# A hybrid decoder block: the mixing stage's first tile and branch weights read in attention's last head, the residual rows read during the last experts

## The chip, the cores and the metric

The kernel runs on one NeuronCore of a Trainium2 chip. The metric is the time of one execution on the device in microseconds, as the median of several runs. The core has five engines that run side by side and meet at semaphores: TensorE (PE; PEld is its weight load), VectorE (DVE), ScalarE (ACT), GpSimd (POOL) and SyncE (SP), which here only issues DMAs.

## The reference

One decoder block on 2048 tokens of width 1024, in f32, followed by a last norm:

```python
h = rmsnorm(x, g_mix)
proj = h @ w_in
attn = mla_attention(...)                 # 8 heads, causal
conv = gated_short_conv(bcx, conv_w)
mixed = g_a * (attn @ w_branch_a) + g_b * (conv @ w_branch_b)
x = x + mixed @ w_out
x = x + memory_cross_attention(rmsnorm(x, g_xattn), rmsnorm(mem, g_mem), ...)
x = x + hierarchical_moe(rmsnorm(x, g_moe), ...)   # 64 experts, two per token
return rmsnorm(x, g_final)
```

## The kernel before

The kernel is a chain of stages, each a block of its own: at its end all engines meet, and the next stage's instructions start together. The stages that matter here are `attention`, `mix`, `experts` and `combine`. Precise products are made of three TensorE products: each operand is cast to a high half (ACT), and the rest is subtracted out as a low half (DVE or POOL); high by high, high by low and low by high are summed in PSUM.

`attention` goes through 8 heads. A head has 40 steps `u`, one tile of scores each (128 keys by up to 512 queries, in four query chunks). Per step TensorE makes the scores three steps ahead and the products with the values two steps behind, ACT makes two exponentials, and DVE (odd steps) or POOL (even steps) subtracts the low half `pl`. In all heads but the last, DVE also finds the maxima of the next head (`top`). ACT copies each finished chunk out of PSUM (`copy_out`, at steps 8, 16, 28 and step 4 of the next head), and SP stores it to `o_d` (values) and `l_d` (row sums) in DRAM. SP's list is in order: the stores, the loads of the next head, the two small writes of the maxima. Before the first head the keys and values of the memory are computed from a 32 KB region per partition (`ea_both`) that `front` had used, and staged through `kmT` and `vm`.

`mix` has 8 chunks of 256 tokens (`CM`). Per chunk TensorE makes 16 groups of 12 products (`branches`, L1139: for each of 8 feature tiles `j` one group with the convolution tile `cT` and `w_branch_b`, one with the attention tile `aT` and `w_branch_a`), then 4 groups of 24 (`output`, L1155, with `w_out`). DVE multiplies each branch group by its gate (L1259) and adds the pair (L1261), ACT casts the sum (L1195), POOL takes its low half (L1225), DVE adds the residual rows (L1270). The attention tile is divided by its row sums (`divide`: a reciprocal of 128x1024 at L1240, a product at L1242), cast by ACT (L1178) and lowered by POOL (L1213). Of the gates four tiles stand in slots, each refilled when its pair is done.

Ahead of the first chunk the weights are brought in: 16 parts of 512 KB (4 of `w_branch_b`, 4 of `w_branch_a`, 8 of `w_out`) go through four staging slots (the halves of `xr` and `xo`). ACT casts each (L1170), DVE lowers the first eight (L1247), POOL the last eight (L1220), and SP issues a part when the slot of the part four before is free. The first convolution, `ar` and `lr` tiles are issued behind part 3, the gates behind part 7, the first residual rows behind part 15. TensorE's first branch group waits for four low halves, the second for eight, the first output group for all of `w_out`.

`experts` goes through 64 experts. The weights of one (two parts of gate and up, one of down, 1 MB each) lie in one of four slots of `raw` (12 MB in all); SP refills the first two parts when DVE has lowered them, the third when the down product is done (L2021). POOL gathers the tokens' rows and scatters the results to `y_d` by indirect DMA (L2061). For the last four experts nothing is refilled.

`combine` goes through 16 tiles of 128 tokens. For each, SP loads the residual rows (512 KB, `cb_xr`, L2301) and the two experts' rows (1 MB, `cb_ys`, L2302) into four slots, and the gain row once, behind the first four pairs. DVE adds both expert rows with their weights (L2345, L2347), ACT squares, sums and takes the root (L2368, L2370), DVE inverts and multiplies (L2352, L2356), SP stores (L2306).

## Time and profile before

| | us |
|---|---|
| median of the runs | 3069.8 (3068.3 to 3072.6) |
| profiled execution | 3075.1 |
| its span | 3073.3 |

| engine | busy us | share |
|---|---|---|
| PE | 2710.8 | 88% |
| DVE | 1604.7 | 52% |
| ACT | 1281.2 | 42% |
| POOL | 627.1 | 20% |

The profile counts time from the start of the span. `attention` ends and `mix` opens at about 1428 us, `mix` ends about 1831, the experts end near 2974 and `combine` runs to the end. A line of the timeline gives the start, the duration, the engine, the line of the kernel, the operation and its operands with their form, how many of them in a row it stands for, and in brackets the idle time before it with the one who ended it. Granted clock and DMA share are given by stretch of time.

### The profile page before, as it was taken

The page shows a single profiled execution, that of the slowest core. Times are in us where ns is not written, and L with a number is a line of the kernel's source. Part 1 is how long each engine was busy: PE and PEld are TensorE (multiplying, and loading weights), DVE is VectorE, ACT ScalarE, POOL GpSimd, SP SyncE. Part 2 cuts the span into 40 slices and gives each one's busy share as a digit, 9 for nine tenths or more (in the row PEclk, how much of TensorE's full clock was granted, in tenths as well). Part 3 has the DMA queues.
Part 4 walks back from the last instruction along what each step waited for, and adds up shares of the span by engine and source line. Part 5 has one row for each costly group of instructions (what it writes and reads, how often), then busy time and mean ns, then how long its engine had stood idle before and what let it go on. Part 6 is the DMA issues. An engine that isn't in the chain of part 4 may idle for free. (4 is left out here: it accounts for less than half of the span.)

```text
span 3073.3 us, 37486 instructions
## 1 busy us (share of the span) xinstructions
PE 2710.8 (88%) x12695; PEld 2070.6 (67%) x12695; DVE 1604.7 (52%) x2108; ACT 1281.2 (42%) x2105; POOL 627.1 (20%) x710
## 2 busy tenths in 40 slices
PE   7999999999979999995899985999729999999960
PEld 5787777777746666664899974777516777666630
DVE  3624525325245666653444423554466777676637
ACT  4334333333317766665211113443205555555524
POOL 0000000000015555553422210000012222344410
PEclk9999999999989999997999996999859999999985
DMA  4353452452531112203544523222256999999958
GB/s 160 99 179 120 134 161 96 163 198 80 179 78 36 39 35 43 56 9 108 162 117 127 150 84 135 74 103 89 83 203 238 361 360 360 359 365 358 349 202 355
DMA packets 168444, 507.57 MB, mean 165 GB/s; under 512 B 40560, under 2 KB 69488, under 8 KB 140176
## 3 DMA queue, kind: packets, MB, share of 16 engines
q1 hardware_dynamic: 149904, 472.59, 44.8%
q0 software_dynamic: 18432, 33.60, 3.0%
q8 instruction: 61, 1.00, 0.1%
q14 instruction: 47, 0.39, 0.0%
HBM read 431.19 MB, written 108.33 MB: 176 GB/s over the span
## 5 line engine op out<-in xcount | busy, mean ns | idle before, releaser
L485 DVE TENSOR_TENSOR fr_wl<-fr_raw,fr_wh 128x1024 fp32r<-128x1024 f32 x128 | 156.8, 1225 | 469.0 <-ACT fr_wh L356 468.6
L2230 DVE TENSOR_TENSOR ex_gl<-ba_raw,ex_gh 128x2048 fp32r<-128x2048 f32 x128 | 290.7, 2291 | 152.7 <-ACT ex_gh L2161 152.7
L356 ACT CAST fr_wh<-fr_raw 128x1024 fp32r<-128x1024 f32 x128 | 134.0, 1047 | 490.6 <-PE fr_acc L280 490.6
L2161 ACT CAST ex_gh<-ba_raw 128x2048 fp32r<-128x2048 f32 x128 | 241.0, 1906 | 95.1 <-DMA ba_raw<-in_w_exp 52.9
L898 ACT ACTIVATE at_pf<-at_psS 128x512 f32<-128x512 f32 (+1 forms) x320 | 178.5, 559 | 168.8 <-PE at_psS L783 86.0
L1006 POOL TENSOR_TENSOR at_pl<-at_pf,at_ph 128x512 fp32r<-128x512 f32 (+1 forms) x160 | 194.8, 1218 | 263.1 <-ACT at_ph L899 262.6
L2125 PE MATMUL ex_psY<-ba_raw,ex_hT 128*128 128x512 f32 x512 | 232.0, 596 | 9.8 <-issue 8.8
L2104 PE MATMUL ex_psG<-ex_gh,ex_xh 128*128 128x512 f32 x512 | 225.6, 441 | 2.9 <-DVE ex_hm L2241 1.4
L969 DVE TENSOR_TENSOR at_pl<-at_pf,at_ph 128x512 fp32r<-128x512 f32 (+2 forms) x160 | 144.1, 904 | 147.8 <-ACT at_ph L899 144.8
L930 DVE TENSOR_REDUCE at_nm<-at_psA 128x1 f32<-128x512 f32 (+2 forms) x320 | 183.1, 605 | 66.5 <-PE at_psA L817 44.0
L2106 PE MATMUL ex_psG<-ex_gh,ex_xl 128*128 128x512 f32 x512 | 201.5, 393 | 0.0
L2105 PE MATMUL ex_psG<-ex_gl,ex_xh 128*128 128x512 f32 x512 | 201.0, 392 | 0.0
L899 ACT ACTIVATE at_ph<-at_psS 128x512 fp32r<-128x512 f32 (+1 forms) x320 | 177.3, 554 | 0.0
L1155 PE MATMUL mx_psO<-mx_wo,mx_mT 128*128 128x512 f32 x768 | 175.6, 389 | 0.0
L982 POOL CAST at_vh<-all_cst 128x32 fp32r<-128x32 f32 x2 | 0.5, 226 | 856.6 <-POOLq L109 856.6
L2125 PEld LDWEIGHTS ex_psY<-ba_raw,ex_hT 128*128 128x128 f32 x512 | 92.2, 190 | 106.0 <-issue 105.8
L1155 PEld LDWEIGHTS mx_psO<-mx_wo,mx_mT 128*128 128x128 f32 x768 | 143.7, 188 | 29.5
L280 PE MATMUL fr_acc<-ea_hh,fr_wh 128*128 128x512 f32 x512 | 137.8, 412 | 2.0 <-DVE ea_hl L503 2.0
L280 PE MATMUL fr_acc<-fr_hh,fr_wh 128*128 128x512 f32 x512 | 137.0, 410 | 2.9 <-DVE fr_wl L485 2.9
L817 PE MATMUL at_psA<-at_kh,at_qh 96*128 96x512 f32 (+2 forms) x320 | 119.8, 431 | 20.6 <-DVE at_nm L930 17.4
L780 PE MATMUL at_psS<-at_qh,at_kh 98*128 98x512 f32 (+1 forms) x320 | 122.9, 384 | 9.7 <-DMA at_qh<-at_ml 7.6
L1139 PE MATMUL mx_psAB<-mx_cT,mx_wb 128*128 128x256 f32 x768 | 105.3, 288 | 27.6 <-POOL mx_cT L1211 19.1
(320 smaller groups left out, 5891.6 us busy)
## 6 DMA issues: line engine op xcount, KB each, us to landing
ba_raw<-in_w_exp SPq DMA_DIRECT2D x192, 1024.0 KB, 18.6
fr_raw<-in_w_slabs SPq DMA_DIRECT2D x128, 512.0 KB, 4.2
gates_d<-fr_gst SPq DMA_DIRECT2D x64, 256.0 KB, 4.6
mx_gt<-gates_d SPq DMA_DIRECT2D x64, 256.0 KB, 5.6
cb_ys<-y_d SPq DMA_DIRECT2D x16, 1024.0 KB, 9.3
xa_xe<-x_d SPq DMA_DIRECT2D x18, 512.0 KB, 5.5
mx_xr<-in_x SPq DMA_DIRECT2D x8, 1024.0 KB, 7.1
x_d<-mx_xo SPq DMA_DIRECT2D x8, 1024.0 KB, 5.1
```

The source lines that it names most:

```text
L280: mm = nc.tensor.matmul(acc[i % 2][:], w[:, i % 2, k, :], h[q % 2][:, k, :], start=(j == 0 and k == 0), stop=(j == 2 and k == KD - 1))
L898: nc.scalar.activation(pf[:, u % PR, off:CH], psS[u % RING][:, off:CH], ACT.Exp)
L899: nc.scalar.activation(ph[:, u % PR, off:CH], psS[u % RING][:, off:CH], ACT.Exp).then_inc(hi, 1)
L930: V.tensor_reduce(nm[:, i, c:c + 1], psA[b][:, 0:w], AX, ALU.max, negate=True).then_inc(a_max, 1)
L1006: G_.tensor_tensor(pl[:, r, off:CH], pf[:, r, off:CH], ph[:, r, off:CH], ALU.subtract).then_inc(lo[0], 1)
L1155: mm = nc.tensor.matmul(psO[n][:], mT[:, x_, k, q * P:(q + 1) * P], wop[:, y_, k, hf * CH:(hf + 1) * CH], start=(k == 0 and i == 0), stop= ...
L2104: nc.tensor.matmul(psG[s][:], xh[:, s, f, :], gh[:, s, i, k, :], start=(f == 0), stop=False)
L2105: nc.tensor.matmul(psG[s][:], xh[:, s, f, :], gl[:, s, i, k, :], start=False, stop=False)
L2106: mm = nc.tensor.matmul(psG[s][:], xl[:, s, f, :], gh[:, s, i, k, :], start=False, stop=(f == KD - 1))
L2125: mm = nc.tensor.matmul(psY[f][:], hT[:, s, k, :], raw[:, r, 2, k * D + f * CH:k * D + (f + 1) * CH], start=(k == 0), stop=(k == 1))
L2161: nc.scalar.copy(gh[:, s, i], raw[:, r, i, :].rearrange("p (k n) -> p k n", k=KD // 2)).then_inc(w_hi, 1)
L2230: V.tensor_tensor(gl[:, s, i], raw[:, r, i, :].rearrange("p (k n) -> p k n", k=KD // 2), gh[:, s, i], ALU.subtract).then_inc(w_lo, 1)
```

## The change

Five things, in one edit:

1. In the last head of `attention` SP reads both branch weights (2 MB each) into `wb_raw` and `wa_raw`, which lie in the 32 KB region that the memory's key and value weights had; then, once the first chunk of the last head is stored, `ar` and `lr` of the first mixing tile, into the place of `kmT` and `vm`. DVE makes the reciprocal in four quarters (steps 24 to 30) and the product (step 32), ACT casts it (step 34), POOL lowers it (step 36) into `aT`, which lies over `memT`.
2. `mix` no longer stages the branch weights: ACT casts them from `wb_raw` and `wa_raw`. The low halves of `w_out` (`wo_lo`) lie in the same 32 KB region, so they wait for the eighth low half.
3. The low halves of `w_out` are made by DVE, one behind each feature tile of the first chunk; ACT casts parts 12 to 15 among its casts of that chunk. The first chunk is written out apart from the loop (`chunks_first`). SP issues the convolution tile first, then parts 8 and 9, the gates, parts 10 and 11, then 12 to 15 as low halves free the slots; the first residual rows and the next chunk's inputs come behind the last low half.
4. In the last three experts SP reads the residual rows of `combine` (8 reads of 1 MB) into slots of `raw` as they come free.
5. `combine` takes the residual rows from there, has six slots for the expert rows and three for the output, loads the gain row behind the first tile, and is written out without loops.

The core of the diff:

```diff
@@ attention, SP
-            head(H - 1, 1, False, False, True)
-            store(H - 1, 3)
+            sp.dma_start(wb_raw[:], w_b.rearrange("(k p) n -> p k n", p=P)).then_inc(mixer["ab_in"], 16)
+            sp.dma_start(wa_raw[:], w_a.rearrange("(k p) n -> p k n", p=P)).then_inc(mixer["ab_in"], 16)
+            store(H - 2, 3)
+            store(H - 1, 0)
+
+            sp.wait_ge(o_st[0], 64 * H)
+            sp.wait_ge(kv_out, 32)
+            sp.dma_start(ar[:], o_d[:, 0:CM].rearrange("(f p) t -> p f t", p=P)).then_inc(mixer["ar_in"], 16)
+            for e in range(2):
+                sp.dma_start(lr[e * VD:(e + 1) * VD, :, :], l_d[e:H:2, 0:CM].unsqueeze(0).broadcast_to([VD, H // 2, CM])).then_inc(mixer["ar_in"], 16)
+            for c in range(1, NC_):
+                store(H - 1, c)
@@ attention, ACT, DVE, POOL
+                    if not more and u == 34:
+                        act.wait_ge(mixer["divided"], 1)
+                        nc.scalar.copy(aT[:, 0], ar[:]).then_inc(mixer["in_hi"], 1)
+                    if not more and u in (24, 26, 28, 30):
+                        f = (u - 24) // 2
+                        dve.wait_ge(mixer["ar_in"], 48)
+                        V.reciprocal(lr[:, f, :], lr[:, f, :]).then_inc(mixer["inverted"], 1)
+                    if not more and u == 32:
+                        dve.wait_ge(mixer["inverted"], 4)
+                        V.tensor_tensor(ar[:], ar[:], lr[:], ALU.mult).then_inc(mixer["divided"], 1)
+                    if not more and u == 36:
+                        pool.wait_ge(mixer["in_hi"], 1)
+                        G_.tensor_tensor(aT[:, 1], ar[:], aT[:, 0], ALU.subtract).then_inc(mixer["a_lo"], 1)
@@ mix, SP
-            for i in range(PARTS):
+            conv(0)
+            for i in range(8, PARTS):
                 if i >= 12:
-                    sp.wait_ge(w_lo_p, i - 11)
+                    sp.wait_ge(w_lo, i - 3)
...
-                if i == 7:
+                if i == 9:
                     for j in range(4):
                         gates(0, j)
...
+                if first:
+
+                    sp.wait_ge(w_lo, PARTS)
+                    xrows(0)
@@ mix, ACT and DVE
+                    if first and 2 <= j < 6:
+                        high(10 + j)
...
+                    if first:
+                        low(8 + j)
@@ experts, SP
+            for j in range(NT // 2):
+                r, i = 1 + j // 3, j % 3
+                e = E - RAW + r
+                if i < 2:
+
+                    sp.wait_ge(w_lo, 2 * e + i + 1)
+                else:
+                    sp.wait_ge(down, e + 1)
+                sp.dma_start(raw[:, r, i, :].rearrange("p (t d) -> p t d", d=D),
+                             x3_d[2 * j * P:2 * (j + 1) * P, :].rearrange("(t p) d -> p t d", p=P)).then_inc(x3_in[j], 16)
@@ combine, SP
-    R = 4
+    R = 6
...
+            load(0)
             sp.dma_start(gb[:], g.broadcast_to([P, D])).then_inc(g_in, 16)
+            for i in range(1, R):
+                load(i)
+            for i in range(NT):
+                if i + R < NT:
+                    load(i + R)
+                store(i)
```

## Rows read from the trace of the kernel before

**Rows 1.** Waits of TensorE, 1425 to 1810: who for whom, us, times, longest

```profile
PE mx_psAB L1139 <- POOL mx_cT L1211: 19.1, 1, 19.1
PE mx_psAB L1139 <- DVE mx_wa L1247: 15.0, 1, 15.0
PE mx_psAB L1139 <- DVE mx_m L1259: 8.5, 1, 8.5
```

**Rows 2.** Timeline of TensorE, mixing: start, duration, line, operands, count, idle before

```profile
1443.58 2.90 PE L1139 MATMUL mx_psAB<-mx_cT,mx_wb 128*128 128x256 f32 x12 [19.14 <-POOL mx_cT L1211]
...
1494.77 21.95 PE L1155 MATMUL mx_psO<-mx_wo,mx_mT 128*128 128x512 f32 x96
1516.56 1.60 PE L1139 MATMUL mx_psAB<-mx_cT,mx_wb 128*128 128x256 f32 x12
```

**Rows 3.** Waits of DVE in `combine`, 2975 to the end, columns as rows 1

```profile
DVE cb_xr L2345 <- DMA cb_gb<-in_g_final: 19.3, 1, 19.3
DVE cb_xr L2345 <- DMA cb_ys<-y_d: 10.0, 12, 1.0
```

**Rows 4.** Stretches: busy per engine (count), then TensorE's clock, DMA share, GB/s

```profile
2955.00:2975.00 20.00, 11.88 (x39) 6.47 (x37) 2.29 (x5) 2.19 (x6) 3.71 (x7) 0.96 0.13 51
2975.00:2994.00 19.00, 0.00 (x0) 0.00 (x0) 0.00 (x0) 1.19 (x1) 0.00 (x0) 0.50 0.90 359
...
3015.00:3060.00 45.00, 0.00 (x0) 0.00 (x0) 35.60 (x37) 18.46 (x33) 0.00 (x0) 0.50 1.02 422
```

**Rows 5.** Timelines of SP, DVE, POOL and TensorE, attention's last head to mixing's start

```profile
1370.25 0.59 SPq L716 DMA_DIRECT2D at_qh<-at_ml  x1
...
1383.92 0.51 SPq L721 DMA_DIRECT2D o_d<-at_ost  x1
...
1404.48 0.69 DVE L969 TENSOR_TENSOR at_pl<-at_pf,at_ph 128x512 fp32r<-128x512 f32 x1 [3.14 <-ACT at_ph L899]
...
1421.02 0.74 POOL L1006 TENSOR_TENSOR at_pl<-at_pf,at_ph 128x256 fp32r<-128x256 f32 x1 [0.72 <-ACT at_ph L899]
...
1423.74 0.28 PE L799 MATMUL at_psO<-at_ph,at_vh 128*66 128x256 f32 x1
...
1428.22 1.20 SPq L1084 DMA_DIRECT2D mx_xr<-in_w_branch_b  x2
```

**Rows 6.** DMA issues of mixing, whole span: count, KB each, median us to landing

```profile
mx_gt<-gates_d SPq DMA_DIRECT2D x64, 256.0 KB, 5.6
...
mx_cv<-conv_d SPq DMA_DIRECT2D x8, 512.0 KB, 5.7
...
mx_lr<-l_d SPq DMA_DIRECT2D x16, 256.0 KB, 9.1
```

**Rows 7.** Timelines of DVE, SP and POOL in mixing's steady chunks

```profile
1675.06 6.54 DVE L1240 RECIPROCAL mx_lr<-mx_lr 128x1024 f32<-128x1024 f32 x1
...
1709.23 0.45 SPq L1062 DMA_DIRECT2D mx_ar<-o_d  x1
...
1729.28 2.40 POOL L1213 TENSOR_TENSOR mx_aT<-mx_ar,mx_aT 128x1024 fp32r<-128x1024 f32 x1 [5.45 <-ACT mx_aT L1178]
```

**Rows 8.** Timelines of DVE and POOL before mixing's first chunk

```profile
1454.66 2.35 DVE L1247 TENSOR_TENSOR mx_wa<-mx_xr,mx_wa 128x1024 fp32r<-128x1024 f32 x2
1456.93 4.50 DVE L1247 TENSOR_TENSOR mx_wa<-mx_xo,mx_wa 128x1024 fp32r<-128x1024 f32 x2
...
1455.90 3.31 POOL L1213 TENSOR_TENSOR mx_aT<-mx_ar,mx_aT 128x1024 fp32r<-128x1024 f32 x1 [12.43 <-ACT mx_aT L1178]
```

**Rows 9.** Line L2061, the last three scatters, 2950 to 2974

```profile
L2061 POOL DMA_INDIRECT y_d<-ex_y,ex_iy x3: 992/993/996, 2955.5 to 2970.1; - x3
...
DMA to landing us min/median/max: 3.2/3.2/3.2
```

**Rows 10.** Line L2061, four scatters among the weight loads, 2900 to 2935

```profile
DMA to landing us min/median/max: 9.0/9.5/10.0
```

**Rows 11.** Timeline of DVE in `combine`, the first sums of two tiles

```profile
3000.95 1.28 DVE L2345 SCALAR_TENSOR_TENSOR cb_xr<-cb_ys,ba_wts,cb_xr 128x1024 f32<-128x1024 f32 x1
...
3004.97 1.28 DVE L2345 SCALAR_TENSOR_TENSOR cb_xr<-cb_ys,ba_wts,cb_xr 128x1024 f32<-128x1024 f32 x1
```

More of the change, by code:

```diff
@@ L22 @@
 CH = 512
+CM = 256
 NC_ = T // CH
@@ L1076, in _, with chunk @@
             sp.sem_inc(stored, 16)
-            for i in range(PARTS):
+            conv(0)
+            for i in range(8, PARTS):
                 if i >= 12:
-                    sp.wait_ge(w_lo_p, i - 11)
-                elif i >= 4:
-                    sp.wait_ge(w_lo_v, i - 3)
+                    sp.wait_ge(w_lo, i - 3)
                 stage, src, _hi, _lo = weight(i)
                 sp.dma_start(stage, src).then_inc(w_in[i % 4], 16)
-                if i == 3:
-                    conv(0)
-                    rows(0)
-                if i == 7:
+                if i == 9:
                     for j in range(4):
                         gates(0, j)
-            sp.wait_ge(w_lo_p, PARTS - 8)
-            xrows(0)
-            def chunk(c, more):
-                here = sp.snap(c + 0) if more else c
-                after = sp.snap(c + 1) if more else None
+            def chunk(c, more, first=False):
+                here = sp.snap(c + 0) if more and not first else c
+                after = sp.snap(c + 1) if more and not first else c + 1
                 for j in range(4):
@@ L1115, in chunk @@
                     xrows(after)
-            chunks(sp, chunk)
+            chunks_first(sp, chunk)
             sp.wait_ge(stored, 16 * NM + 16)
@@ L1144, in output @@
                 if first:
-                    pe.wait_ge(w_lo_p, PARTS - 8)
+                    pe.wait_ge(w_lo, PARTS)
                 for n in range(2 * NQ):
@@ L1184, in _, with chunk @@
                 high(i)
-            attention_high(0)
-            for i in range(8, PARTS):
+            for i in range(8, 12):
                 high(i)
-            def chunk(c, more):
+            def chunk(c, more, first=False):
                 for j in range(KD):
@@ L1200, in chunk @@
                     attention_high(c + 1)
-            chunks(act, chunk)
+            chunks_first(act, chunk)
         @block.gpsimd
@@ L1215, in _ @@
             pool.sem_inc(m_lo, 2)
-            inputs(0)
-            for i in range(8, PARTS):
-                pool.wait_ge(w_hi, i + 1)
-                stage, _src, hi, lo = weight(i)
-                G_.tensor_tensor(lo, stage, hi, ALU.subtract).then_inc(w_lo_p, 1)
+            conv_low(0, 2)
             def chunk(c, more):
@@ L1240, in divide, with low, chunk @@
                 V.reciprocal(lr[:], lr[:]).then_inc(inverted, 1)
-                dve.wait_ge(inverted, c + 1)
+                dve.wait_ge(inverted, c + 4)
                 V.tensor_tensor(ar[:], ar[:], lr[:], ALU.mult).then_inc(divided, 1)
-            for i in range(8):
+            def low(i):
                 dve.wait_ge(w_hi, i + 1)
                 stage, _src, hi, lo = weight(i)
-                V.tensor_tensor(lo, stage, hi, ALU.subtract).then_inc(w_lo_v, 1)
-                if i == 3:
-                    divide(0)
-            def chunk(c, more):
+                if i == 8:
+                    dve.wait_ge(w_lo, 8)
+                V.tensor_tensor(lo, stage, hi, ALU.subtract).then_inc(w_lo, 1)
+            for i in range(8):
+                low(i)
+            def chunk(c, more, first=False):
                 for j in range(KD):
@@ L1964, in _, with experts @@
             link(V.tensor_copy(meta[:, 0:32], psK[0:1, 0:32]))
-def experts(nc, cst, h_d, w_exp, y_d, tab, rows, meta, raw, r_in):
+def experts(nc, cst, h_d, x3_d, w_exp, y_d, tab, rows, meta, raw, r_in, x3_in):
     with ExitStack() as ctx:
@@ L2362, in _ @@
             act.wait_ge(eps_set, 1)
[L2363 to L2370 removed]
+            for i in range(NT):
+                act.wait_ge(added, i + 1)
+                if i >= 2:
+                    act.wait_ge(rcp_done, i - 1)
+                nc.scalar.activation(sq[:], x_tile(i), ACT.Square, accum_out=st[:, i % 2, 0:1]).then_inc(sq_done, 1)
+                act.wait_ge(sq_done, i + 1)
+                nc.scalar.activation(st[:, i % 2, 1:2], st[:, i % 2, 0:1], ACT.Sqrt, bias=eps[:], scale=1.0 / D).then_inc(rms_done, 1)
 def program(nc, a, out):
@@ L2407, in program @@
                   a["mem"], a["g_mem"], a["w_kv_mem"], hh0, hl0, wk_mem, wv_mem, memT, kv_in)
-            attention(nc, cst, qn_d, qr_d, kn_d, kr_d, v_d, o_d, l_d, wk_mem, wv_mem, memT, kv_in, km_d, vm_d)
-        mix(nc, o_d, l_d, conv_d, gates_d, x, a["w_branch_a"], a["w_branch_b"], a["w_out"], x2_d)
+            at = -(-nc.sbuf_base // 32) * 32
+            kmT, vm = e_.sb("kmT", [P, XH, MEM]), e_.sb("vm", [P, MEM // P, XH * XD])
+            ar, lr = (e_.at(n, [P, 4, CM], F32, at + 4 * 4 * CM * i) for i, n in enumerate(("ar", "lr")))
+            attention(nc, cst, qn_d, qr_d, kn_d, kr_d, v_d, o_d, l_d, wk_mem, wv_mem, memT, kmT, vm, kv_in, km_d, vm_d,
+                      a["w_branch_a"], a["w_branch_b"], wb_raw, wa_raw, ar, lr, aT, mixer)
+            mix(nc, o_d, l_d, conv_d, gates_d, x, a["w_out"], x2_d, wb_raw, wa_raw, wo_lo, ar, lr, aT, mixer)
         clear_semaphores(nc)
@@ L2432, in program @@
             route(nc, cst, lg, wts, tab, rows, meta, load_first_experts)
-            experts(nc, cst, h_d, a["w_exp"], y_d, tab, rows, meta, raw, r_in)
-            combine(nc, x3_d, y_d, wts, a["g_final"], out)
+            x3_in = [b_.sem(f"x3_in{i}") for i in range(NT // 2)]
+            experts(nc, cst, h_d, x3_d, a["w_exp"], y_d, tab, rows, meta, raw, r_in, x3_in)
+            combine(nc, raw, x3_in, y_d, wts, a["g_final"], out)
 def constants():
```

140 lines of the change are left out of this document (66 added, 74 removed).

## The prediction

> **What bounds the kernel now.** I read the waits first, then the timeline where they are long. In the mixing stage TensorE stands still three times, 19.1, 15.0 and 8.5 us, and never again [rows 1]: first for POOL's low half of the convolution tile, then for DVE's low halves of `w_branch_a`, then for DVE's `mx_m`, which itself was held by POOL working through the low halves of `w_out`. TensorE's groups show it: the first twelve products at 1443.58, the first output products at 1494.77, the second chunk at 1516.56 [rows 2]; from there the stage runs on TensorE without a gap. In `combine` DVE waits 19.3 us once, for the gain row that is queued behind four pairs of loads, then 10.0 us in twelve waits for the expert rows [rows 3]. The DMA share by stretch says why: 0.13 in the last 20 us of the experts, then 0.90 and 1.02 [rows 4]. So both ends of this change aim at time in which TensorE or DVE really waits. The profiled execution took 3075.1 us (span 3073.3); the median of the runs is 3069.8, 5.3 below it. I sum in the profile's clock and take the gain off the median.
>
> **Part 1, the last head of attention.** Added there: on SP two reads of 2 MB (the branch weights), one read of `ar`, two of `lr`; on DVE four reciprocals of a quarter each and one product; on ACT one cast; on POOL one subtraction. SP issues the weights behind the maxima of head 7, at 1370.9 [rows 5]. At 359 GB/s [rows 4] 4.2 MB take 12 us, so they are in by 1383. Head 6's last store, now queued behind them, lands about then; ACT needs it only at step 16 of the head, near 1392. The chain that matters: the first store of head 7 is issued at 1383.9 [rows 5], SP waits for its landing (about 3 us), then issues `ar` and `lr`, whose median landing is 9.1 us [rows 6], so about 1398. DVE asks for them behind step 23, about 1401, and its next piece of attention work starts at 1404.48 after 3.14 us of idle [rows 5]: a quarter of the reciprocal (6.54 us whole [rows 7]), 1.6 us, fits in. The later gaps on DVE are about as wide. ACT's cast and DVE's product lie two units of work or more ahead of TensorE. Only POOL is tight: its subtraction of 2.40 us [rows 7] comes behind step 36 and ahead of its last piece, which ran at 1421.02 for 0.74 us; it now ends near 1423.5, and TensorE starts those products at 1423.74 [rows 5]. I take a loss of 0.5 us (0 to 3). Cover gone: any lateness of the read beyond 1404.5 stops DVE, and with it TensorE, one for one.
>
> **Part 2, the start of mixing.** The block opens at 1428.22 as before [rows 5]. ACT casts the four parts of `w_branch_b` at once (about 1 us each), waits for the convolution tile, now the first DMA, landing 5.7 us after issue [rows 6], so 1434, then casts `w_branch_a`. DVE's low halves take 1.18 us each (two in 2.35) [rows 8]. While POOL subtracts the convolution tile DVE is held for about 1.4 us, so the eighth low half is done near 1442. TensorE's first group starts near 1438.5 at the lower clock (2.90 us against 1.60 for twelve products [rows 2]), its second at 1442 instead of 1461.5. From then on a pair of groups takes 2.9 us, and DVE has per pair two products, one sum and now one low half, about 2.5 us: it keeps up until the fourth pair.
>
> Then a new wait. SP issues `w_out` parts 12 to 15 only as the low halves 8 to 11 free the slots, one per pair, and only behind part 15 the gates of pair 4. The pairs end at 1443.9, 1446.8, 1449.7 and 1452.6, and the sum and low half of the fourth take 2.4 us more, so with SP's issues that is near 1455.5; the gates land 5.6 us after issue [rows 6], so 1461.1, while DVE wants them at 1455.6. From there DVE sets the pace: two products, one sum (about 1.15 us together), one low half (1.2 us) and what POOL's subtraction costs it. The rows for that: two low halves that met a POOL subtraction took 4.50 us instead of 2.35, and POOL's took 3.31 us instead of 2.40 [rows 7, 8]. Each held the other. Here POOL's piece is about 0.7 us long and has to wait for ACT's cast, while DVE's low half starts right behind the sum; so DVE mostly goes first, and between nothing and 0.7 us I take 0.1. Four pairs of 2.45 us give 9.8 us: all sixteen low halves are done at 1471, and the output products start there, not at 1494.77. TensorE idles about 4.5 us before them; I charge 1 us for the low clock (0 to 1.5, half of a cold 2.90).
>
> The Trainium skill (SBUF — State Buffer, section "Who interferes with whom") says that a DVE instruction with two SBUF inputs and a POOL instruction that reads SBUF exclude each other, and that the later one waits the whole earlier one out. If POOL came first in all four pairs, that rule would make this sum 2.5 us longer; the rows above agree with it in kind.
>
> **Part 3, the second chunk's inputs.** They move behind that new wait too: SP may fetch the x rows, then `conv`, `ar`, `lr` only once all low halves are done. In steady state 22.4 us pass from the issue of `ar` (1709.23) to the end of POOL's low half (1731.68) [rows 7]. Here 0.9 us of other issues and 1 MB of x rows (2.9 us at 359 GB/s) come on top: 1471 + 26.2 = 1497.2. TensorE ends the output products 21.8 us [rows 2] plus the 1 us after 1471, at 1493.8, and needs the half one group later, 1495.3. A new stall of about 1.8 us (0 to 4). Gain of the stage: 1516.6 - 1493.8 - 1.8 = 21 us; with the gates in time it is 27, with both chains at their long ends 13. The seven later chunks are the same code.
>
> **Part 4, the residual rows.** Eight reads of 1 MB go out when slots of the last three experts come free: two near 2933, three near 2953.6, three near 2963.6, into a DMA that is 0.13 busy [rows 4]; nothing of the experts' own weights is behind them. What they meet is POOL's scatter. It lands 3.2 us after issue when alone [rows 9], 9.5 under full weight traffic [rows 10]. The last three megabytes are through by about 2974, so the last scatter (issued at 2970) shares only part of its time: I take 1.5 us on the end of the block (0 to 6.3). The Trainium skill (DMA: Bandwidth & Descriptors, "Queues, rings and completion order") says that each DMA engine takes turns between queues by the packet. With turns the scatter pays the 1.5; without them it would stand behind the reads, at most 3.
>
> **Part 5, combine.** The first expert rows are now alone in front: issue 2976.3, landing about 4.8 us later, 2981.1; the gain row and the second tile (1.5 MB, 4.2 us) give 2985.3, where DVE waits 1.6 us. Against 2994.0 (2974.7 + 19.3 [rows 3]) that is 11.3 us. Then each tile needs 1.5 MB instead of 2: at 422 GB/s [rows 4] 3.7 us, below DVE's own 4.02 us a tile (3000.95 to 3004.97 [rows 11]), so the twelve waits, 10.0 us, go. Straight code drops the register work of a loop; I take 1.5 us (0 to 2). ACT's two table loads stay beside the start. Gain 11.3 + 10.0 + 1.5 = 22.8, call it 23. What is late next is DVE.
>
> **Sum.** 21 + 23 - 0.5 = 43.5 us: 3031.6 on the profile's scale, 3026 against the median.
>
> **Rivals.** (a) The gates are no wait: they come in time because DVE is later or because they land in 3 us. Mixing gains 26: 3021. For it: two parts of `w_out` may have drained by then. Against: they stand last in SP's order. Chance 0.13. (b) `combine` turns DMA-bound: reads and stores mixed move 360 GB/s as in the read-only stretch, 4.37 us a tile, 15 x 0.35 = 5 us lost: 3031. Against it stands the 422 of the same loop. Chance 0.14. (c) Mixing keeps a long start: DVE, which now has all sixteen low halves, loses the full POOL time and the second chunk's inputs come late; gain 13: 3034. Chance 0.10. (d) The change does less than it says: both (b) and (c), with 6 us on the last scatter: 3045. Chance 0.05. (e) Slower: the read of `ar` and `lr` in the last head. SP waits for a store that stands behind 4 MB, and DVE waits for the read with TensorE's products behind it. Each us beyond 1404.5 costs one; the gain is eaten when the read lands later than 1447, 60 us after its issue. At 1460 it gives 3082. Rows show 9.1 us for such a read, so 0.04, a fifth of it landing near no change.
>
> **Chances.** Forecast 0.54. Cases (a), (b), (c) and the forecast hold 0.91; with the unknown costs at their ends they reach from 3015 to 3040, which I give as the range. A measurement of this kernel can tell some 0.2%, 6 us. Faster 0.95, same 0.01, slower 0.04.
>
> **What would show it.** In the profile after: the first TensorE group of mixing near 1438, the second near 1442; a DVE wait for `mx_gt` of some 5 us near 1456; first output products near 1471; a wait of TensorE for POOL's `mx_aT` near 1496. In `combine`, no wait for the gain row, first sum about 6.5 us after the block opens, DVE back to back at 4 us a tile. Wrong would be: waits of DVE for `at`'s read in the last head, waits for the expert rows on most tiles, or the last scatter landing more than 5 us after issue.

## The result, and the profile after

The changed kernel takes 3022.6 us (median of four runs, 3015.9 to 3024.7) against 3070.2 us (3068.3 to 3072.6) beside it on the same chip: a ratio of 0.985, 95% interval 0.983 to 0.986, so 47.7 us faster. The forecast was 3026 (3015 to 3040). The profiled execution took 3024.7 us, its span is 3022.9.

The first lines of its page: TensorE is busy for as long as before (2707.9 us against 2710.8) in a shorter span.

```profile
span 3022.9 us, 37234 instructions
## 1 busy us (share of the span) xinstructions
PE 2707.9 (90%) x12695; PEld 2067.9 (68%) x12695; DVE 1611.0 (53%) x2119; ACT 1270.1 (42%) x2098; POOL 607.0 (20%) x702
```

The waits of TensorE from 1365 to 1560 (for whom, us, times, longest), the answer to [rows 1]:

```profile
PE mx_psAB L1165 <- POOL mx_cT L1240: 11.4, 1, 11.4
PE mx_psAB L1165 <- DVE mx_m L1291: 2.5, 1, 2.5
PE mx_psO L1181 <- DVE ea_wo_lo L1278: 2.1, 1, 2.1
PE mx_psAB L1165 <- DVE mx_wa L1278: 1.5, 1, 1.5
```

The timeline of TensorE behind it, the answer to [rows 2]: first group, second group, first output products, second chunk.

```profile
1435.05 2.90 PE L1165 MATMUL mx_psAB<-mx_cT,mx_wb 128*128 128x256 f32 x12 [11.41 <-POOL mx_cT L1240]
1439.49 2.93 PE L1165 MATMUL mx_psAB<-ea_aT,mx_wa 128*128 128x256 f32 x12 [1.54 <-DVE mx_wa L1278]
...
1469.44 0.73 PE L1181 MATMUL mx_psO<-mx_wo_hi,mx_mT 128*128 128x512 f32 x2 [2.11 <-DVE ea_wo_lo L1278]
...
1492.95 1.59 PE L1165 MATMUL mx_psAB<-mx_cT,mx_wb 128*128 128x256 f32 x12
1494.82 1.70 PE L1165 MATMUL mx_psAB<-ea_aT,mx_wa 128*128 128x256 f32 x12 [0.27 <-POOL ea_aT L1246]
```

The wait of 15.0 us for `w_branch_a` is 1.5, the one of 8.5 for `mx_m` is 2.5. The block now opens at 1427.10, so the second chunk starts 65.9 us behind the opening instead of 88.3 (1516.56 less 1428.22 in [rows 2, 5]). The new waits stand on DVE: timeline, the gates of pair 4, the place where they were issued on SP, and the first reads for the second chunk.

```profile
1459.36 0.76 DVE L1291 TENSOR_TENSOR mx_m<-mx_psAB,mx_gt 128x256 f32<-128x256 f32 x2 [5.75 <-DMA mx_gt<-gates_d]
...
1454.01 1.97 SPq L1100 DMA_DIRECT2D mx_gt<-gates_d  x4
1469.41 0.37 SPq L1103 DMA_DIRECT2D mx_xr<-in_x  x1
1469.83 0.46 SPq L1097 DMA_DIRECT2D mx_cv<-conv_d  x1
1470.34 0.50 SPq L1091 DMA_DIRECT2D ea_ar<-o_d  x1
```

In `combine` the wait for the gain row is gone, and where twelve waits for the expert rows stood, two are left, for the first two tiles. One part of this is DVE's own: before, it waits for the gain row ahead of its first sum; in the changed kernel this wait stands ahead of the first multiplication by the gain, where the row is already in (it landed 6.5 us after its issue). In the changed kernel ACT also writes the squares out in bf16; DVE has no wait for ACT in either profile beyond 0.2 us. Waits and timeline of DVE, the answers to [rows 3, 11] (the two last lines are two tiles of the loop in a row, 3.91 us apart):

```profile
DVE ba_raw L2377 <- DMA cb_ys<-y_d: 6.6, 2, 5.0
...
2955.20 1.28 DVE L2377 SCALAR_TENSOR_TENSOR ba_raw<-cb_ys,ba_wts,ba_raw 128x1024 f32<-128x1024 f32 x1 [4.96 <-DMA cb_ys<-y_d]
2959.49 1.28 DVE L2377 SCALAR_TENSOR_TENSOR ba_raw<-cb_ys,ba_wts,ba_raw 128x1024 f32<-128x1024 f32 x1 [1.68 <-DMA cb_ys<-y_d]
...
2971.23 1.28 DVE L2377 SCALAR_TENSOR_TENSOR ba_raw<-cb_ys,ba_wts,ba_raw 128x1024 f32<-128x1024 f32 x1
...
2975.14 1.28 DVE L2377 SCALAR_TENSOR_TENSOR ba_raw<-cb_ys,ba_wts,ba_raw 128x1024 f32<-128x1024 f32 x1
```

By stretch (columns as [rows 4]): the last experts, the start of `combine`, its loop. DVE is busy 52.0 of 53 us in the loop. The landing of the last three scatters stands below them; the last one took 7.2.

```profile
2925.00:2950.00 25.00, 13.46 (x45) 7.75 (x43) 3.13 (x6) 2.68 (x6) 4.08 (x9) 0.84 0.81 295
2950.00:2962.00 12.00, 0.00 (x0) 0.00 (x0) 5.10 (x5) 2.73 (x4) 0.00 (x0) 0.50 0.91 339
2962.00:3015.00 53.00, 0.00 (x0) 0.00 (x0) 52.04 (x56) 20.22 (x42) 0.00 (x0) 0.50 0.91 379
...
DMA to landing us min/median/max: 7.2/8.0/8.3
```

Put end to end, the two profiled executions differ by 50.4 us, and this is where:

| stretch | before | after | gained |
|---|---|---|---|
| up to the issue of the maxima in the last head | 1370.25 | 1369.32 | 0.9 |
| from there to the opening of `mix` | 57.97 | 57.78 | 0.2 |
| opening to the second chunk, with the wait for `aT` | 88.3 | 66.1 | 22.2 |
| rest of mixing | 327.5 | 327.8 | -0.3 |
| cross attention up to the first expert | 461.3 | 458.8 | 2.5 |
| experts, first to last products | 659.2 | 656.3 | 2.9 |
| last scatter's issue to the opening of `combine` | 4.64 | 8.46 | -3.8 |
| `combine`, opening to the last multiplication | 94.2 | 68.5 | 25.7 |

The places that the change touches make 44.0 us; 6.3 lie in stretches that it doesn't touch.

### The profile page after: what moved, and what is told of

Read it like the earlier page. It is cut to its first block and busy times, and to the rows that moved or that the text cites. A ratio compares the mean times of both kernels' runs of the same rounds, so it can differ in the third digit from the quotient of the medians.

```text
span 3022.9 us, 37234 instructions
## 1 busy us (share of the span) xinstructions
PE 2707.9 (90%) x12695; PEld 2067.9 (68%) x12695; DVE 1611.0 (53%) x2119; ACT 1270.1 (42%) x2098; POOL 607.0 (20%) x702
## 3 DMA queue, kind: packets, MB, share of 16 engines
q1 hardware_dynamic: 149680, 472.59, 45.6%
## 5 line engine op out<-in xcount | busy, mean ns | idle before, releaser
L1181 PE MATMUL mx_psO<-mx_wo_hi,mx_mT 128*128 128x512 f32 x512 | 159.0, 392 | 2.1 <-DVE ea_wo_lo L1278 2.1
L281 PE MATMUL fr_acc<-fr_hh,fr_wl 128*128 128x512 f32 x512 | 126.9, 390 | 0.0
L281 PE MATMUL fr_acc<-ea_hh,fr_wl 128*128 128x512 f32 x512 | 126.8, 390 | 0.0
```

The source lines that it names most:

```text
L281: mm = nc.tensor.matmul(acc[i % 2][:], w[:, i % 2, k, :], h[q % 2][:, k, :], start=(j == 0 and k == 0), stop=(j == 2 and k == KD - 1))
L1181: mm = nc.tensor.matmul(psO[n][:], mT[:, x_, k, q * P:(q + 1) * P], wop[y_][:, k, hf * CH:(hf + 1) * CH], start=(k == 0 and i == 0), stop= ...
```

## The experiments

### The two halves apart

`mix_only` keeps the changes of attention and mixing and has the old end of the experts and the old `combine`:

```diff
@@ experts, SP
-            for j in range(NT // 2):
...
-                sp.dma_start(raw[:, r, i, :].rearrange("p (t d) -> p t d", d=D),
-                             x3_d[2 * j * P:2 * (j + 1) * P, :].rearrange("(t p) d -> p t d", p=P)).then_inc(x3_in[j], 16)
@@ combine
-def combine(nc, raw, x3_in, y_d, wts, g, out):
-    R = 6
+def combine(nc, x3_d, y_d, wts, g, out):
+    R = 4
```

> The changed attention and mixing with the experts and combine of before. My theory: the two ends of the change are independent, so this keeps the gain of mixing alone, 22.5 us between the opening of mixing and the second chunk in the two profiles: 3047 us. Rival: part of that gain comes from what the other end does (or drifts with it), then the two halves don't add up to the whole, and this run lies nearer 3040 or nearer 3055.

`combine_only` is the other half: the old attention and `mix` with the new reads in the experts and the new `combine`.

```diff
@@ attention and mix
-            sp.dma_start(wb_raw[:], w_b.rearrange("(k p) n -> p k n", p=P)).then_inc(mixer["ab_in"], 16)
-            sp.dma_start(wa_raw[:], w_a.rearrange("(k p) n -> p k n", p=P)).then_inc(mixer["ab_in"], 16)
...
-def mix(nc, o_d, l_d, conv_d, gates_d, x, w_out, x2_d, wb_raw, wa_raw, wo_lo, ar, lr, aT, mixer):
+def mix(nc, o_d, l_d, conv_d, gates_d, x, w_a, w_b, w_out, x2_d):
```

> The attention and mixing of before with the changed experts and combine. Theory: combine, from its opening to the end, takes 73 us instead of 98.6, and the last scatter lands 4 us later than before (7.2 us after issue instead of 3.2): gain 22 us, 3048. Rival: the scatter's lateness and other waits in the last experts cost more, gain under 15 us.

Measured beside the kernel before at 3068.4: 3046.7 (ratio 0.993, 0.991 to 0.995) and 3043.7 (0.992, 0.990 to 0.994), 21.7 and 24.7 us faster, together 46.4 of the 47.7. The halves add within what such medians scatter; no sign is left that one feeds on the other. `combine_only` shows the slower scatter too (8.8 us from its issue to the next block), `mix_only` does not (5.5).

### The place of the gates

`gates_early` issues each of the four last gates behind its part of `w_out`:

```diff
                 sp.dma_start(stage, src).then_inc(w_in[i % 4], 16)
+                if i >= 12:
+                    sp.wait_ge(gated, 2 * (i - 12) + 6)
+                    gates(0, i - 8)
...
-                for j in range(4):
+                for j in range(0 if first else 4):
```

> The changed kernel, but in mixing's first chunk SP issues the gates of pairs 4 to 7 one behind each of the w_out parts 12 to 15, not all behind part 15. Theory: the DVE wait of 5.75 us for the gates goes, DVE and TensorE run on at 2.9 us a pair, the output products start 4 us earlier (near 38.3 us after the opening of mixing, not 42.3), and about 2 us of it come back as a wait for POOL's half of the second attention tile, whose inputs arrive as late as before after the last low half. Gain 2 to 4 us on the changed kernel. Rival: DVE is the bound anyway because of its low halves, the output products start as before, no gain.

3018.6 us (3017.1 to 3025.3), 4 below the changed kernel, on another chip and with ranges that overlap, so the trace has to tell. The wait of DVE for the gates is gone, TensorE's for `mx_m` with it, and the output products start 37.9 us behind the opening instead of 42.3. Of these 4.4 us, 2.0 stand as a wait a step later, and behind it TensorE runs at its lower clock (granted 0.62 from 1489.7 to 1494.2; twelve products take 2.65 us instead of 1.60), some 1.6 us more. From the opening to its last product the stage is 2.8 us shorter than in the first profile of the changed kernel and 2.3 shorter than in the second:

```profile
PE mx_psO L1184 <- DVE ea_wo_lo L1281: 2.1, 1, 2.1
PE mx_psAB L1168 <- POOL ea_aT L1249: 2.0, 1, 2.0
...
1489.73 2.65 PE L1168 MATMUL mx_psAB<-ea_aT,mx_wa 128*128 128x256 f32 x12 [2.04 <-POOL ea_aT L1249]
```

The second chunk's inputs still hang on the last low half, and the output products no longer cover them. `inputs_early` is the same kernel with those reads ahead of that wait:

```diff
+                if more:
+                    sp.wait_ge(c_lo, c + 1)
+                    conv(after)
+                    sp.wait_ge(a_lo, c + 1)
+                    rows(after)
                 if first:
                     sp.wait_ge(w_lo, PARTS)
                     xrows(0)
-                if more:
-                    sp.wait_ge(c_lo, c + 1)
-                    conv(after)
-                    sp.wait_ge(a_lo, c + 1)
-                    rows(after)
```

> The kernel with the gates of the last four pairs issued between the parts of w_out, and besides the second chunk's convolution and attention reads ahead of the wait for the last low half. If TensorE's 2.0 us of waiting for the second attention tile there came from the place of these reads behind that wait: it goes, and the stage is 2 us shorter still, 5 to 6 us below the changed kernel. The rival, that the reads land as late as before behind the last parts of w_out, or delay those: no more gain than the gates alone, 3 us.

It ran beside the changed kernel, taken once more:

> The changed kernel itself, unaltered, beside the three others on one chip: 3020 to 3026. It also gives a second profile of the stages that the change does not touch: if the 5 us by which cross attention and the experts were shorter in the first one are the scatter of one execution, they come out elsewhere this time; if they belong to the changed kernel, they come back the same.

The changed kernel again: 3022.2 us (ratio 0.986, 0.984 to 0.987). Cross attention takes 457.0 us and the experts 656.7, near the 458.8 and 656.3 of its first profile; by my own test they would then belong to the changed kernel, but `gain_first`, which has none of the change in these places, took 458.0 and 654.9, so the test doesn't decide it. `inputs_early`: 3011.5 (3010.3 to 3018.2; ratio 0.983, 0.981 to 0.985). In its waits nothing of the second chunk is left, and the second chunk stands 59.8 us behind the opening (1483.96 less 1424.21) against 65.9, or 63.9 with 1.7 of waiting, in the two profiles of the changed kernel:

```profile
PE mx_psAB L1169 <- POOL mx_cT L1244: 11.4, 1, 11.4
PE mx_psO L1185 <- DVE ea_wo_lo L1282: 2.1, 1, 2.1
PE mx_psAB L1169 <- DVE mx_wa L1282: 1.5, 1, 1.5
...
1483.96 1.60 PE L1169 MATMUL mx_psAB<-mx_cT,mx_wb 128*128 128x256 f32 x12
1485.40 1.60 PE L1169 MATMUL mx_psAB<-ea_aT,mx_wa 128*128 128x256 f32 x12
```

So the first theory holds with some 6 us. The medians differ by 10.7; the other 4 to 5 us lie in the experts (652.0 us from first to last products against 656.7), which this edit doesn't touch, and the intervals of the two ratios overlap. I credit the edit with 6, which is also what the stage from its opening to its last product gains (373.7 us against 380.3 and 379.8).

### What the prepared tile is worth

`tile_in_mix` leaves only the branch weights in the last head; the tile is divided and split in `mix` again.

```diff
@@ attention, SP, ACT, DVE, POOL
-            sp.dma_start(ar[:], o_d[:, 0:CM].rearrange("(f p) t -> p f t", p=P)).then_inc(mixer["ar_in"], 16)
...
-                        V.reciprocal(lr[:, f, :], lr[:, f, :]).then_inc(mixer["inverted"], 1)
...
-                        G_.tensor_tensor(aT[:, 1], ar[:], aT[:, 0], ALU.subtract).then_inc(mixer["a_lo"], 1)
@@ mix, SP, DVE
             conv(0)
+            rows(0)
...
+                if i == 3:
+                    divide(0)
```

> The changed kernel with the first tile prepared in the mixing stage again; only the branch weights stay in the last head. If the prepared tile is worth what it looks like: the read of ar and lr lands some 11 us after the block opens, the four reciprocals (4 x 1.75 us) and the product stand on DVE between the low halves, and TensorE's second group starts 10 to 12 us later than the 12.4 us after opening of the changed kernel; the stage loses about as much, 8 to 12 us (3031 to 3035 against 3023). The rival, that the weights of the first pair set the pace and the tile would be ready anyway: under 2 us lost.

3037.0 us (ratio 0.991, 0.989 to 0.992): 14.4 lost, more than expected. The second group waits 16.4 us instead of 1.5 and starts 27.2 us behind the opening (12.4), the output products 56.5 (42.3). The timeline of DVE and then of TensorE:

```profile
1438.24 6.55 DVE L1252 RECIPROCAL ea_lr<-ea_lr 128x1024 f32<-128x1024 f32 x1 [7.01 <-DMA ea_lr<-l_d]
...
1445.97 6.78 DVE L1262 TENSOR_TENSOR mx_wa<-ea_wa,mx_wa 128x1024 fp32r<-128x1024 f32 x4
...
1452.81 2.93 PE L1148 MATMUL mx_psAB<-ea_aT,mx_wa 128*128 128x256 f32 x12 [16.37 <-DVE mx_wa L1262]
...
1482.08 1.15 PE L1164 MATMUL mx_psO<-mx_wo_hi,mx_mT 128*128 128x512 f32 x2 [2.69 <-DVE ea_wo_lo L1262]
```

The divide stands in the middle of DVE's list. DVE waits 7.0 us for its read and works 7.8 us on it, and the low halves of `w_branch_a` come after both: 14.8 us, the delay of the second group to the tenth. I had counted the work and only part of the wait. Of the 22 us of the mixing stage, the tile carries 14 as long as the rest of the change is in place.

### Who makes the low halves of `w_out`

`lows_on_pool` gives them back to POOL, with ACT's casts ahead of the first chunk:

```diff
@@ mix, ACT
-            for i in range(8, 12):
+            for i in range(8, PARTS):
@@ mix, DVE
-                    if first:
-                        low(8 + j)
@@ mix, POOL
+            for i in range(8, PARTS):
+                pool.wait_ge(w_hi, i + 1)
+                stage, _src, hi, lo = weight(i)
+                if i == 8:
+                    pool.wait_ge(w_lo, 8)
+                G_.tensor_tensor(lo, stage, hi, ALU.subtract).then_inc(w_lo, 1)
```

> The changed kernel with eight of the sixteen low halves of w_out on POOL and their casts on ACT, as before the change; the early weights and the early tile stay. If the split of the low halves matters by itself: POOL needs about 8 x 2.5 us from 14 us after opening, DVE's products of the pairs 2 and on wait for POOL's low half of m, and the output products start 8 to 11 us later than the 42.3 us after opening (3031 to 3034). The rival, that DVE with one low half a pair costs as much as it saves: within 2 us of the changed kernel.

3026.6 us (0.986, 0.984 to 0.987): 4 lost against the first median of the changed kernel, between the two bounds. In the trace the stage, from its opening to its last product, is only 1.5 us longer (381.7 against 380.3) or 2.0 (against 379.8), which is what the rival said. POOL works through the low halves until 1460.9, and the wait of 8.5 us of [rows 1] is back, to the tenth:

```profile
PE mx_psAB L1165 <- DVE mx_m L1295: 8.5, 1, 8.5
...
1456.32 4.64 POOL L1253 TENSOR_TENSOR ea_wo_lo<-mx_xo,mx_wo_hi 128x1024 fp32r<-128x1024 f32 x2
1460.92 1.41 POOL L1257 TENSOR_TENSOR mx_mT<-mx_m,mx_mT 128x256 fp32r<-128x256 f32 x2
```

But the output products start only 3.7 us later (46.0 behind the opening), and the second chunk 2.0 us. I had added POOL's time to the changed kernel's start and left out that the wait replaces two others: the one for the gates, which here are in before DVE needs them, and the 2.1 us for the last low half.

### The read in the last head, delayed

`late_read` tests the rival that ended on the slow side: the weights are read behind the first store of head 7, twice, with a wait between, so `ar` and `lr` come late.

```diff
@@ attention, SP
-            sp.dma_start(wb_raw[:], w_b.rearrange("(k p) n -> p k n", p=P)).then_inc(mixer["ab_in"], 16)
-            sp.dma_start(wa_raw[:], w_a.rearrange("(k p) n -> p k n", p=P)).then_inc(mixer["ab_in"], 16)
             store(H - 2, 3)
             store(H - 1, 0)
             sp.wait_ge(o_st[0], 64 * H)
             sp.wait_ge(kv_out, 32)
+            for rd in range(2):
+                if rd:
+                    sp.wait_ge(mixer["ab_in"], 32 * rd)
+                sp.dma_start(wb_raw[:], w_b.rearrange("(k p) n -> p k n", p=P)).then_inc(mixer["ab_in"], 16)
+                sp.dma_start(wa_raw[:], w_a.rearrange("(k p) n -> p k n", p=P)).then_inc(mixer["ab_in"], 16)
```

> The changed kernel with the branch weights read behind the first store of head 7 and read twice, with a wait between, so that the read of ar and lr in the last head lands about 24 us later than the 1393 of the changed kernel, near 1418. If each us past the point where DVE wants it costs one: DVE waits about 13 us for it, TensorE's attention products behind it as well, 12 to 16 us lost (3035 to 3039). The rival, that the queued products of the two units in flight cover most of it: at most 5 us lost.

3034.0 us (0.989, 0.988 to 0.991), 11.4 lost, just under the 12 to 16. DVE waits 18.0 us for the read, TensorE 12.4:

```profile
1417.53 1.75 DVE L992 RECIPROCAL ea_lr<-ea_lr 128x256 f32<-128x256 f32 x1 [18.01 <-DMA ea_lr<-l_d]
...
1419.88 0.69 PE L812 MATMUL at_psO<-at_ph,at_vh 128*66 128x512 f32 x1 [12.36 <-DVE at_pl L985]
1420.37 0.63 PE L813 MATMUL at_psO<-at_pl,at_vh 128*66 128x512 f32 x1
...
1425.23 0.40 PE L813 MATMUL at_psO<-at_pl,at_vh 128*66 128x512 f32 x1
```

5.6 of the 18.0 us are covered by the products that TensorE had queued. Then it runs at its lower clock for 5 us: 12 products stand 0.43 us apart instead of 0.23, 2.3 us more. 12.4 + 2.3 = 14.7, and the block opens 14.8 us later, counted from the issue of the maxima (72.6 against 57.8). Mixing takes 3.2 of it back: 1.7 by the fourth group, since TensorE comes to its second group at the full clock (granted 1.00 from 1453.4, 1.70 us for twelve products instead of 2.93), the rest in the later waits and in the output products. Why the clock was back sooner here, no run shows.

### `combine`: the gain row, the slots

`gain_first` is the kernel before with one read moved:

```diff
-            for s in range(R):
-                load(s, s)
+            load(0, 0)
             sp.dma_start(gb[:], g.broadcast_to([P, D])).then_inc(g_in, 16)
+            for s in range(1, R):
+                load(s, s)
```

> The kernel before, with the gain row of combine read behind the first pair of loads instead of behind four. If the wait of 19.3 us was only the place in the queue: DVE's first normalized tile starts 12 us earlier, and since the loop is then bound by the reads (2 MB a tile at 422 GB/s are 4.97 us against 4.02 of DVE), only part reaches the end: 5 to 11 us gained (3059 to 3065 against 3070). The rival, that transfers were the bound all along: the same bytes move in the same time, under 3 us gained.

3057.6 us beside 3066.7 (ratio 0.996, 0.995 to 0.998). The block takes 85.2 us from its opening to the last multiplication instead of 94.2. The wait for the gain row falls from 19.3 to 7.9, the waits for the expert rows grow to 12.5, and the loop moves its 2 MB a tile at the rate of [rows 4]:

```profile
DVE cb_xr L2346 <- DMA cb_ys<-y_d: 12.5, 13, 2.1
DVE cb_xr L2346 <- DMA cb_gb<-in_g_final: 7.9, 1, 7.9
...
2990.00:3040.00 50.00, 0.00 (x0) 0.00 (x0) 39.39 (x41) 22.16 (x37) 0.00 (x0) 0.50 1.02 421
```

`four_slots` is the changed kernel with `R = 4` in `combine` for `R = 6`.

> The changed kernel with four slots for pairs of expert rows in combine instead of six. If the waits of before came from the bytes (2 MB a tile, now 1.5 MB): DVE goes on back to back at 3.91 us a tile and the time is within 1 us of the changed kernel. The rival, that the deeper queue removed them: waits for the expert rows return, up to 10 us lost.

3024.4 us (0.986, 0.984 to 0.988), 2.2 above the changed kernel beside it, but not by this block: in the profile `combine` takes 68.5 us, as with six. No wait for the expert rows beyond the first two tiles:

```profile
DVE ba_raw L2377 <- DMA cb_ys<-y_d: 6.7, 2, 4.8
```

So of the 25.7 us of this block, 9 are the place of the gain row alone, and the deeper queue isn't needed for the rest. That leaves 16.7 for the residual rows gone from the block (1.5 MB a tile for 2), for DVE's later wait for the gain row, for the third output slot and for the code without loops. Of these the loops are worth some 1.6 us, 15 tiles by the 0.11 between 4.02 and 3.91; no run takes the other three apart.

### The residual reads beside the scatter

`last_rows_late` moves three of the eight reads into `combine`, behind the first six loads:

```diff
@@ experts, SP
-            for j in range(NT // 2):
+            for j in range(5):
@@ combine, SP
             for i in range(1, R):
                 load(i)
+            for j in range(5, NT // 2):
+                sp.dma_start(raw[:, 1 + j // 3, j % 3, :].rearrange("p (t d) -> p t d", d=D),
+                             x3_d[2 * j * P:2 * (j + 1) * P, :].rearrange("(t p) d -> p t d", p=P)).then_inc(x3_in[j], 16)
```

> The changed kernel, but the last three of the eight reads of residual rows are issued in combine behind the first six tiles of expert rows, not in the last expert. Theory: the last scatter is alone again and lands 3.2 us after issue instead of 7.2, combine opens 4 us earlier, and the three megabytes are in long before tile 10 needs them: gain 4 us. Rival: they push the reads of expert rows out, DVE waits on tiles 6 to 9, and 4 or more us are lost again.

3023.8 us (0.987, 0.984 to 0.989): nothing gained, and in the trace of the two blocks 3.8 lost. The scatter is fast again, 5.2 us from its issue (2936.02) to the next block (2941.24), 3.2 less than in the changed kernel. But `combine` takes 75.6 us for 68.5. The expert rows, which the rival named, are no later than before (6.5 us in two waits); one store lands late and DVE waits for its slot:

```profile
2944.75 3.14 SPq L2362 DMA_DIRECT2D ba_raw<-x_d  x3
...
2972.16 1.28 DVE L2393 SCALAR_TENSOR_TENSOR cb_yo<-ba_raw,cb_st,cb_gb 128x1024 f32<-128x1024 f32 x1 [7.22 <-DMA out<-cb_yo]
```

`rows_spread` is `inputs_early` with two reads moved, one at a time:

```diff
@@ experts, SP
-            for j in range(NT // 2):
+            for j in range(6):
@@ combine, SP
                 store(i)
+                if i in (2, 6):
+                    j = 6 + i // 6
+                    sp.dma_start(raw[:, 1 + j // 3, j % 3, :].rearrange("p (t d) -> p t d", d=D),
+                                 x3_d[2 * j * P:2 * (j + 1) * P, :].rearrange("(t p) d -> p t d", p=P)).then_inc(x3_in[j], 16)
```

> As the run before it, and the last two of the eight reads of residual rows are issued in combine behind the third and the seventh store, so that only one read stands beside the last scatter. If it is those reads that slow the scatter, and it was their burst that delayed the first stores when three were moved at once: scatter 8.5 us from issue to the next block becomes 5.5 to 7, and the loop keeps 3.91 us a tile with no wait for stores, 1.5 to 3 us gained over inputs_early. The rival: the reads beside the loop (2 MB a tile in two places) bring back a wait of DVE for stores of 3 us or more, nothing gained or a loss.

3016.7 us (0.983, 0.982 to 0.985). Again the scatter is 5.2 us (8.8 in `inputs_early`), and again a wait for stores eats it:

```profile
DVE cb_yo L2398 <- DMA out<-cb_yo: 3.3, 2, 1.8
```

The rival holds: 3.7 us less at the scatter, 3.3 more in `combine`. Those two megabytes cost about the same on either side of the block's end. The loop's DMA share was 0.91 without them; why two reads hold up a store there, no run shows. The median is 5 us above `inputs_early`, but in its profile the last head is already reached 6.1 us later (1372.49 against 1366.42 at the issue of the maxima), in code that is the same.

## Why the prediction was right, step by step

**The last head** was sized right: 0.5 us forecast, none measured (57.8 us for 58.0). By the timeline DVE's first quarter of the reciprocal starts at 1400.34 without waiting, the four take 1.75 us each, and POOL's subtraction (1419.38, 2.71 us) ends as its last piece begins (1422.06). `late_read` gives the one-for-one price of rival (e) in the number: I had let the loss begin 34.2 us behind the issue of the maxima (1404.5 less 1370.3); there DVE begins 49.1 us behind it, 14.9 later, and the block opens 14.8 later. The mechanism was not that, though: TensorE stood only 12.4 us, since products in its queue covered part of DVE's wait, and the lower clock behind the stall added 2.3. That the two cancel is luck. The read itself has room: issued at 1385.9, it lands about 1394.

**The start of mixing** went as told, each mark within 2.3 us and the output products within 0.5: first group 8.0 us behind the opening (forecast 10.3; ACT began to cast the convolution tile 3.7 us after the opening, where I had let it land 5.7 us after its issue), second group 12.4 (13.8), wait for the gates 5.75 (5.5), output products 42.3 (42.8). Between the second group and the gates two errors cancel: that group came 1.4 us earlier than told, but it and half of the third ran at the lower clock (granted 0.50 from 1439.4 to 1441, 0.59 from there to 1444), where I had all behind the first at the full one; the fourth pair ends 24.3 us behind the opening (24.4). `gates_early` shows what this wait is worth: 4.4 us at the output products, 2.3 to 2.8 at the end of the stage, less than the 5 that rival (a) gave it, since the second chunk's inputs and the clock take the rest back. (a) itself didn't happen, and (c) and (d) neither. The gain of the stage was 22.2 us against 21. The sum of (d) is a slip: both (b) and (c) with 6 us on the scatter give 3043.5, since 1.5 of the 6 were already in the forecast.

**POOL beside DVE.** The pieces of POOL in the first chunk took 1.21 us instead of 0.74, and DVE's low halves 1.22, no more than alone: DVE went first each time, as forecast, and lost nothing. Where POOL went first, DVE was held:

```profile
1428.11 4.63 DVE L1278 TENSOR_TENSOR mx_wb<-ea_wb,mx_wb 128x1024 fp32r<-128x1024 f32 x4 [5.87 <-ACT mx_wb L1199]
1432.85 6.59 DVE L1278 TENSOR_TENSOR mx_wa<-ea_wa,mx_wa 128x1024 fp32r<-128x1024 f32 x4
...
1431.94 3.01 POOL L1240 TENSOR_TENSOR mx_cT<-mx_cv,mx_cT 128x1024 fp32r<-128x1024 f32 x1 [9.10 <-ACT mx_cT L1203]
...
1461.09 1.21 POOL L1253 TENSOR_TENSOR mx_mT<-mx_m,mx_mT 128x256 fp32r<-128x256 f32 x1 [6.88 <-ACT mx_mT L1223]
```

Four low halves beside POOL's convolution tile took 1.96 us more than four alone; the last line is a piece of the first chunk, with DVE first. With the rule of the Trainium skill (SBUF — State Buffer, "Who interferes with whom"), that the later of the two waits the earlier one out, both cases agree in kind; the 2.5 us that it would have cost with POOL first in all four pairs did not come, since the order was the other.

**The second chunk's inputs**: 1.8 us forecast, 0.3 and 1.7 in the two profiles of the changed kernel, 2.0 in `gates_early`. The first two differ by the clock: in the first profile TensorE falls to the lower one in the output products (granted 0.72 from 1469 to 1475), they take 23.5 us and cover the wait; in the second they take 21.9 at the full clock, and the wait is there. I had charged 1 us for the clock and 1.8 for the wait; together they came to 2.0 and 1.8, for 2.8.

**The scatter** is the step whose size was wrong: 1.5 us forecast, 3.8 measured, and 3.5 to 4.2 in each of the nine runs with all eight reads. Its landing of 7.2 us was also one of my signs of being wrong (more than 5), and it lies between the 3.2 of [rows 9] and the 9.0 to 10.0 under weight traffic of [rows 10]. Nearly all of the reads were through by 2946, 4.4 us after the scatter's issue, where I had said 4. The step that failed is the share: I let the scatter pay only part of that time. The queues from its issue to its landing, 2941.6 to 2949.2 (packets, MB, share), and below them those of the kernel before, 2970 to 2974:

```profile
q1 hardware_dynamic: 381, 1.43, 46.4%
q0 software_dynamic: 286, 0.67, 22.3%
...
q0 software_dynamic: 144, 0.33, 20.9%
```

q1 are SP's reads, q0 the scatters. A scatter alone moves 0.33 MB; here q0 moves twice that, since the scatter before it (issued at 2936.96) lands only after 8.3 us, at 2945.3, where it had been alone with its 3.2 in the kernel before. So 1.43 MB of reads and 0.34 of the other scatter go through first or beside it: by my estimate 4.3 us at the 408 GB/s measured from 2941.6 to 2944, against the 4.0 by which the landing is longer. Both queues move bytes all the while. With the turns between queues that the Trainium skill states (DMA: Bandwidth & Descriptors, "Queues, rings and completion order") this agrees: from 2941.6 to 2943 q1 moves 0.34 MB and q0 0.21. But the scatter's last bytes came behind nearly all of the others, and neither of the two prices that I gave, 1.5 us and at most 3, was enough.

**`combine`** gained 25.7 us between its opening and its end, 24.4 by the working. Its marks: first sum 5.1 us behind the opening (my 6.5 counted from the old opening, and so held the scatter's 1.5 as well), wait for the second tile 1.68 (1.6), then 3.91 us a tile instead of 4.02 and no waits. Rival (b) is out: DVE went on without waits, at 379 GB/s over the stretch. The errors, -2.3 on the scatter, +1.3 here and +1.2 in mixing, cancel almost wholly; that the places touched came to 44.0 us against 43.5 is in part luck.

**What the working doesn't cover** is 6.3 us in stretches with the same code. Cross attention up to the first expert took 461.3 us in the profile of before, 461.0 in `combine_only` and 458.0 in `gain_first`, both with the old mixing; the experts took 659.2, 658.4 and 654.9. In the eleven other profiles they took 457.0 to 460.5 and 652.0 to 657.4. So these stretches vary by 4 and 7 us from one profile to the next, and the way to the last head's maxima by 6.5 (1366.0 to 1372.5). The sums of the two overlap, 1112.9 to 1120.5 us with the old mixing and 1109.7 to 1116.2 with the new. The profiled execution of before, 5.3 us above its median, had drawn long ones. Forecasting from its clock and taking the gain off the median left that out, and the medians (47.7, and 45.6 in the repeat, against 44.0 in the touched places) say that this was nearly right. Whether 2 us of the rest belong to the change stays open.

## What to carry to other kernels

A short wait at a stage's start is worth removing in the order of SP's list first: the gates and the second chunk's inputs stood behind transfers that needed a slot, and moving issues alone gave some 6 us more. Before moving reads into a quiet stretch, look at what lands at its end: here the scatter paid for them, with nearly all the time that the bytes still in flight took, and moving them behind it cost as much in the stores. When a step is taken out of one engine's list, count the wait it brings as well: the divide was worth 14.8 us, 7.8 of its own work and 7.0 for its read.

## What the runs showed of the hardware

- The last indirect scatter took 4.6 to 5.5 us from its issue to the next block with none of the last three reads of 1 MB issued ahead of it, 5.2 with one of them, and 8.1 to 8.9 with all three: one costs nothing that can be seen, three cost 3 to 4 us.
- In `combine`, three extra reads of 1 MB held DVE for 7.2 us behind a late store, two spread ones for 3.3; by an estimate from the 422 GB/s of [rows 4], a megabyte takes 2.5 us.
- After a stall of 12.4 us TensorE made twelve products at 1.2 GHz (granted clock 0.51 from 1419 to 1425, then 1.00), which cost 2.3 us on top of the stall. After a wait of only 2.0 us in `gates_early` it fell to 1.2 GHz as well (0.62 from 1489.7 to 1494.2), after one of 1.7 in the second profile of the changed kernel it did not. All kernels stood 11.4 us or more before mixing's first group and made it at 1.2 GHz; `late_read` alone made its second group at 2.4 GHz (1.70 us), the others at 1.2 GHz (2.93).
